# Cross attention: scaled negative queries, row minimum and exponential read from PSUM, eight score buffers, one loop over both head pairs

## The reference

```python
def memory_cross_attention(xn, memn, wq, wk, wv, wo):
    q = (xn @ wq).reshape(B, S, N_CROSS_HEADS, CROSS_HEAD_DIM)
    k = (memn @ wk).reshape(B, M, N_CROSS_HEADS, CROSS_HEAD_DIM)
    v = (memn @ wv).reshape(B, M, N_CROSS_HEADS, CROSS_HEAD_DIM)
    s = jnp.einsum('bshd,bmhd->bhsm', q, k) * (CROSS_HEAD_DIM ** -0.5)
    p = jax.nn.softmax(s, axis=-1)
    o = jnp.einsum('bhsm,bmhd->bshd', p, v).reshape(B, S, CROSS_WIDTH)
    return o @ wo
```

## Time and profile before

| | |
|---|---|
| median of 3 runs | 3515.47 us (3515.1 to 3517.26) |
| the profiled execution | 3516.87 us, its span 3515.6 us |
| TensorE busy, share of the span | 3219.0 us, 92% |
| VectorE, ScalarE, GpSimd busy | 42%, 29%, 21% |
| mean granted TensorE clock | 0.959 |

### The profile page before, as it was taken

How to read it: one execution, slowest core, us unless ns; L and a number is a source line. 1 busy time by engine, 2 the same in 40 slices (tenths; PEclk the granted TensorE clock), 3 DMA queues, 4 the chain that set the end, 5 groups by cost and what they waited for, 6 DMA issues and landing times.

```text
span 3515.6 us, 32414 instructions
## 1 busy us (share of the span) xinstructions
PE 3219.0 (92%) x12964; PEld 2212.1 (63%) x12964; DVE 1462.6 (42%) x2389; ACT 1023.5 (29%) x1679; POOL 752.2 (21%) x448
## 2 busy tenths in 40 slices
PE   6998888888899899999998799999988699999997
PEld 6444446655544788888886344486433488888886
DVE  4234443333217445545546544574223233333334
ACT  0223443334202222222223550063333422222223
POOL 0300002211005344444443110101000322222221
PEclk9999999989999999999999899999998799999998
DMA  6210001111114111111112102001300111111111
GB/s 199 84 31 24 24 30 32 41 36 54 72 61 149 36 60 48 48 48 48 48 48 81 39 24 74 30 3 44 108 24 25 53 54 48 48 48 48 48 48 54
DMA packets 195427, 187.25 MB, mean 53 GB/s; under 512 B 16119, under 2 KB 143503, under 8 KB 195279
## 3 DMA queue, kind: packets, MB, share of 16 engines
q1 hardware_dynamic: 195279, 185.19, 16.8%
HBM read 173.34 MB, written 9.70 MB: 52 GB/s over the span
## 4 chain that ended last, share of the span: by engine, by line
PE 82%; ACT 7%; DVE 6%; issue 3%; POOL 1%; SPq 1%; DMA 0%; POOLq 0%; ACTq 0%; DVEq 0%
PE bank L1026 62%; PE bank L1052 5%; PE bank L1122 2%; PE bank L1346 2%; PE bank L994 1%; PE bank L1330 1%; PE bank L1179 1%; PE bank L1300 1%; PE bank L1322 1%; PE bank L991 1%; PE bank L1188 1%; PE bank L989 1%; PE bank L1013 1%; PE bank L1389 1%; PE bank L1319 1%
## 5 line engine op out<-in xcount | busy, mean ns | idle before, releaser
L1026 PE MATMUL bank<-ft,panel 128*128 128x512 f32 x896 | 389.9, 596 | 7.5 <-ACT ft L2202 4.1
L1026 PEld LDWEIGHTS bank<-ft,panel 128*128 128x128 f32 x896 | 171.0, 192 | 222.9 <-issue 222.9
L1026 PE MATMUL bank<-ft_hi,panel_hi 128*128 128x512 f32 x704 | 278.2, 395 | 13.9 <-POOL ft_lo L2601 9.3
L1026 PE MATMUL bank<-ft_hi,panel_lo 128*128 128x512 f32 x704 | 278.4, 395 | 0.0
L1026 PE MATMUL bank<-ft_lo,panel_hi 128*128 128x512 f32 x704 | 277.4, 394 | 0.0
L2545 POOL TENSOR_TENSOR panel_lo<-panel,panelm_hi 128x1024 fp32r<-128x1024 f32 x64 | 153.1, 2393 | 508.1 <-ACT panelm_hi L2165 508.1
L1052 PE MATMUL bank<-ft,panel 128*128 128x512 f32 x512 | 245.0, 620 | 4.0 <-ACT z L2291 2.7
L1881 DVE TENSOR_SCALAR ffn_conv<-ffn_in,ffn_taps 128x512 f32<-128x512 f32 x88 | 113.0, 1284 | 316.1 <-ACT ffn_in L2408 316.1
L2132 DVE TENSOR_TENSOR resid<-resid,bank 128x512 f32<-128x512 f32 x256 | 174.5, 686 | 151.5 <-PE bank L1026 150.7
L1026 PE MATMUL bank<-ftm_hi,panelm_hi 128*128 128x512 f32 x512 | 203.3, 397 | 23.1 <-issue 12.9
L2545 POOL TENSOR_TENSOR panel_lo<-panel,panel_hi 128x1024 fp32r<-128x1024 f32 x66 | 157.9, 2400 | 248.0 <-ACT panel_hi L2165 248.0
(11 more groups left out here) (433 smaller groups left out, 5726.2 us busy)
## 6 DMA issues: line engine op xcount, KB each, us to landing
panel<-in_w_ada SPq DMA_DIRECT2D x48, 512.0 KB, 3.7
panel<-in_w_in SPq DMA_DIRECT2D x48, 512.0 KB, 3.7
panel<-in_ffn_w_up SPq DMA_DIRECT2D x44, 512.0 KB, 3.8
panel<-in_w_mlp_in SPq DMA_DIRECT2D x32, 512.0 KB, 4.1
panel<-in_w_mlp_out SPq DMA_DIRECT2D x32, 512.0 KB, 3.6
panel<-in_w_o SPq DMA_DIRECT2D x24, 512.0 KB, 3.6
panel<-in_w_out SPq DMA_DIRECT2D x24, 512.0 KB, 3.6
panel<-in_ffn_w_down SPq DMA_DIRECT2D x22, 512.0 KB, 3.5
```

Of the source, the lines that this page charges most:

```text
L1026: m = te.matmul(ps, a, b, start=(start and j == 0), stop=(stop and j == len(pairs) - 1))
```

## The change

The queries are multiplied by -1/sqrt(128) when they leave their banks, so the banks of `c_score` hold the negated, scaled scores. VectorE takes the row minimum directly from the bank, and this is the bias; the instruction that negated the maximum is gone. ScalarE's exponential reads the bank, with scale -1, writes the buffer and frees the bank; the instruction that copied and scaled the scores is gone. There are eight `c_scores` buffers. Scores are issued five steps ahead, finishes two steps ahead. Scores take banks 0 to 3, turns 4 and 5, weighings 6 and 7. The second half's scores and finishes are issued within the last steps of the first, and the first half's last weighing stands behind the turn of the second half's step 1.

```diff
@@ -40,6 +40,7 @@
 CROSS = 4
 NFF2 = 4096 // P
 AHEAD = 2
+C_AHEAD = 5
 SLOTS = 6
 SPLITS = 3
 
@@ -570,28 +571,35 @@
             k.unit("project", "cq", c, h, ps[c], used=ps[c], last=("cq", c, h))
             if h == 0 and c in (1, 2):
                 f3[c - 1]()
+
+    def c_score(i, u):
+        k.banks.take(("c_score", i, u), (0, 1, 2, 3))
+        k.unit("c_score", i, u, 2 * i + u // NT, u % NT)
+
+    def c_weigh(i, u):
+        k.banks.take(("c_weigh", i, u), (6, 7))
+        k.unit("c_weigh", i, u, 2 * i + u // NT, u // 4 % 2)
+
     for i in range(CROSS // 2):
-        def c_score(u):
-            k.banks.take(("c_score", i, u))
-            k.unit("c_score", i, u, 2 * i + u // NT, u % NT)
-
-        def c_weigh(u):
-            k.banks.take(("c_weigh", i, u))
-            k.unit("c_weigh", i, u, 2 * i + u // NT, u // 4 % 2)
-
-        for u in range(3):
-            c_score(u)
-        k.unit("c_finish", i, 0)
+        if i == 0:
+            for u in range(C_AHEAD):
+                c_score(i, u)
+            k.unit("c_finish", i, 0)
+            k.unit("c_finish", i, 1)
         for u in range(2 * NT):
-            if u < 2 * NT - 3:
-                c_score(u + 3)
-            if u < 2 * NT - 1:
-                k.unit("c_finish", i, u + 1)
-            k.banks.take(("c_turn", i, u))
+            later = (i, u + C_AHEAD) if u + C_AHEAD < 2 * NT else (i + 1, u + C_AHEAD - 2 * NT)
+            if later[0] < CROSS // 2:
+                c_score(*later)
+            soon = (i, u + 2) if u + 2 < 2 * NT else (i + 1, u + 2 - 2 * NT)
+            if soon[0] < CROSS // 2:
+                k.unit("c_finish", *soon)
+            k.banks.take(("c_turn", i, u), (4, 5))
             k.unit("c_turn", i, u)
             if u % 4 == 1 and u > 4:
-                c_weigh(u - 5)
-        c_weigh(2 * NT - 4)
+                c_weigh(i, u - 5)
+            elif u == 1 and i:
+                c_weigh(i - 1, 2 * NT - 4)
+    c_weigh(CROSS // 2 - 1, 2 * NT - 4)
     f1, a1 = feats("norm_mlp", range(4), ring), applies("norm_mlp", (0, 1, 2, 3))
     f2, a2 = feats("norm_mlp", (4, 5), ring), applies("norm_mlp", (4, 5))
     f3, a3 = feats("norm_mlp", (6, 7), ring), applies("norm_mlp", (6, 7))
@@ -696,7 +704,7 @@
     k.params, k.npar = place("params", [P, 4, 11]), place("npar", [P, 4, 2])
     k.lam, k.lam_sp = place("lam", [P, 8]), place("lam_sp", [P, 8])
     k.inv_freq = place("inv_freq", [P, 1])
-    k.c_stat = place("c_row_stat", [P, 4, 4])
+    k.c_stat = place("c_row_stat", [P, C_AHEAD + 3, 4])
     first_panel = top
     k.panels = [place(f"panel{n}", [P, D]) for n in range(SLOTS)]
     rows = top
@@ -802,7 +810,7 @@
     k.k_mem, k.v_mem = place("k_mem", [P, CROSS, MEM], at=late), place("v_mem", [P, MEM // P, BANK], at=late + 4 * D)
     k.mem_t, k.mem_ft = place("mem_t", [P, MEM // P, D], at=at(20)), place("mem_ft", [P, KD, MEM], at=at(22))
     top = at(12)
-    k.c_scores = [place(f"c_scores{n}", [P, MEM]) for n in range(4)]
+    k.c_scores = [place(f"c_scores{n}", [P, MEM]) for n in range(C_AHEAD + 3)]
     k.p_tc = [place(f"p_tc{n}", [P, MEM // P, BANK]) for n in range(2)]
 
 
@@ -1376,7 +1384,7 @@
         pe.wait_ge("c_weights_done", i, u)
         ps = free("c_turn", i, u)
         for kk in range(2):
-            m = te.transpose(ps[:, tile(kk)], k.c_scores[u % 4][:, tile(kk)], k.ident[:])
+            m = te.transpose(ps[:, tile(kk)], k.c_scores[u % len(k.c_scores)][:, tile(kk)], k.ident[:])
         fill(m, "c_turn", i, u)
 
     def c_weigh(i, u0, head, hf):
@@ -2087,15 +2095,13 @@
                                 ALU.add), "out_turn", pair, hf, 1)
 
     def c_score(i, u, head, n):
-        s, st = k.c_scores[u % 4], k.c_stat[:, u % 4, :]
+        st = k.c_stat[:, u % len(k.c_scores), :]
+        v.wait_ge(*v.filled("c_score", i, u))
+        dve.tensor_reduce(st[:, 0:1], v.bank("c_score", i, u)[:, 0:MEM], AX, ALU.min).then_inc(*v.new("c_least", i, u))
+
+    def c_finish(i, u):
+        st = k.c_stat[:, u % len(k.c_scores), :]
         v.wait_ge(*v.evicted("c_score", i, u))
-        dve.tensor_reduce(st[:, 0:1], s[:], AX, ALU.max).then_inc(*v.new("c_max", i, u))
-        v.wait_ge("c_max", i, u)
-        dve.tensor_scalar(st[:, 1:2], st[:, 0:1], -1.0, None, ALU.mult).then_inc(*v.new("c_bias", i, u))
-
-    def c_finish(i, u):
-        st = k.c_stat[:, u % 4, :]
-        v.wait_ge("c_exp", i, u)
         dve.reciprocal(st[:, 3:4], st[:, 2:3]).then_inc(*v.new("c_over", i, u))
 
     def c_turn(i, u):
@@ -2265,7 +2271,7 @@
             evict(act.activation(k.gate[h][:], ps[:], ACT.Silu), stage, c, h)
         elif stage == "cq":
             a.wait_ge(*a.filled(stage, c, h))
-            evict(act.copy(k.mix2[:, c, half(h)], ps[:]), stage, c, h)
+            evict(act.mul(k.mix2[:, c, half(h)], ps[:], -float(P) ** -0.5), stage, c, h)
 
     def ada_out(i, n, as_row):
         if as_row and i not in (GT_A, GT_F):
@@ -2488,16 +2494,16 @@
         evict(act.copy(k.k_mem[:, c, :], a.bank("ck", c)[:, 0:MEM]), "ck", c)
 
     def c_score(i, u, head, n):
-        s, st = k.c_scores[u % 4], k.c_stat[:, u % 4, :]
-        if i or u > 3:
-            a.wait_ge(*a.filled("c_turn", *((i, u - 4) if u > 3 else (i - 1, u + 12))))
-        a.wait_ge(*a.filled("c_score", i, u))
-        evict(act.mul(s[:], a.bank("c_score", i, u)[:, 0:MEM], float(P) ** -0.5), "c_score", i, u)
-        a.wait_ge("c_bias", i, u)
-        act.activation(s[:], s[:], ACT.Exp, bias=st[:, 1:2], accum_out=st[:, 2:3]).then_inc(*a.new("c_exp", i, u))
+        s, st = k.c_scores[u % len(k.c_scores)], k.c_stat[:, u % len(k.c_scores), :]
+        depth = len(k.c_scores)
+        if i or u >= depth:
+            a.wait_ge(*a.filled("c_turn", *((i, u - depth) if u >= depth else (i - 1, u + 2 * NT - depth))))
+        a.wait_ge("c_least", i, u)
+        evict(act.activation(s[:], a.bank("c_score", i, u)[:, 0:MEM], ACT.Exp, bias=st[:, 0:1], scale=-1.0,
+                             accum_out=st[:, 2:3]), "c_score", i, u)
 
     def c_finish(i, u):
-        s, st = k.c_scores[u % 4], k.c_stat[:, u % 4, :]
+        s, st = k.c_scores[u % len(k.c_scores)], k.c_stat[:, u % len(k.c_scores), :]
         a.wait_ge("c_over", i, u)
         act.activation(s[:], s[:], ACT.Copy, scale=st[:, 3:4]).then_inc(*a.new("c_weights_done", i, u))
 
```

## The result

| | before | after |
|---|---|---|
| median of 4 runs each, same chip | 3515.28 us (3514.61 to 3517.26) | 3469.27 us (3465.34 to 3471.08) |
| the profiled execution | 3516.87 us, span 3515.6 | 3471.08 us, span 3469.8 |
| first score to first w_co | 2601.70 to 2689.55, 87.85 us | 2600.34 to 2645.59, 45.25 us |
| behind it, to the end of the span | 826.05 us | 824.21 us |
| mean granted TensorE clock | 0.959 | 0.964 |

The ratio is 0.9867 [0.985, 0.9884]: 46.0 us less by the medians, 45.8 by the two profiled executions. Of these 45.8, 42.6 lie in the stage, 1.84 behind it and 1.36 ahead of it, where the kernels differ only in the scaling of the queries. Two more profiles of the kernel after start the stage at 2597.54 and 2601.78, so the 1.36 lies within what one kernel varies by.

A forecast was written before the change was run, and what follows sets the result against it. The cross attention stage was taken as bound by a chain of hand-overs, 1.93 us a step on ScalarE; 42.3 us off the stage plus 1.0 from the clock, 43.3 in total, gave 3473 us, range 3464 to 3486.

The forecast's parts named there:

- The round: In the cross attention's loop, four steps from one weighing to the next would take 5.17 us.
- The ends: Outside the stage's full rounds: 8.6 us to the first weighing, a last round of 4.67, an end of 6.4.
- The two unseen prices: In the stage, instructions reading PSUM that no earlier row showed: exponential taken at 0.50 us, minimum at 0.42.
- The cause of the wait: In each round, VectorE's copy of a weighing's result, waiting for TensorE, holds up the next minimum; round 0.88 us over TensorE's own.
- TensorE's 4.29: In the stage, TensorE's own need for four steps with their weighing at full clock: 4.29 us.
- Nor does a turn's bank: In the loop, turns' banks would not bind: turn 8 needs turn 6's copy, which ends ahead of multiplication 8.
- VectorE's 4.65: In the stage, VectorE's need for four steps, at most 4.65 us, with durations in place of distances.
- Rival 1: In the stage, TensorE is the bound: six rounds of 4.29 us, about 3466 us; chance 0.12.
- The clock: Behind the stage, mostly at w_co's start, denser TensorE work would win back 1.0 of up to 3.3 us.
- Rival 2: TensorE runs at the low clock level in the stage: rounds of 8.58 us, total 3498; chance 0.13.
- Rival 3: In the loop, hand-overs still alternate because only four banks hold scores: step 1.93 us, about 3515; chance 0.04.
- Rival 4: Slower: TensorE's low clock level lasts from the stage into w_co, about 3552 us if through all of it; chance 0.03.

The follow-up runs named there:

- experiment 4: The kernel after with VectorE's copy of a weighing's result issued a step later, behind the next minimum and next turn's copy: 3473.3 us, one execution.
- experiment 5: The kernel after with finishes issued three steps ahead instead of two: 3465.86 us, ratio 0.9858; on another chip 3464.55 us, ratio 0.9849.
- experiment 2: The kernel after with the old instructions (scaling copy, maximum, negation), so the new order alone: 3494.37 us, ratio 0.9945.
- experiment 1: The kernel before with the new instructions alone, keeping its old leads, four buffers and the break between the halves: 3482.61 us, ratio 0.991.
- experiment 3: The kernel after with the break between the halves put back, as two loops: 3470.04 us, ratio 0.9872.
- experiment 7: The kernel after with scores three steps ahead instead of five and six score buffers instead of eight: 3467.39 us, ratio 0.9858.

## Why the prediction was right

It said 3473.0 us; 3469.27 was measured, inside the range of 3464 to 3486 and on the side said likeliest.

**The stage.** 42.3 us less was said, 42.6 came. The round was said to take 5.17 and took 5.17. Term by term, predicted / measured in the timeline shown above: weighing to its copy 1.93 / 1.92; the copy 0.61 / 0.61; minimum to exponential 0.46 / 0.50; exponential, multiplication, exponential 1.40 / 0.47 + 0.40 + 0.45 = 1.32; multiplication to turn 0.56 / 0.55; turn to weighing 0.21 / 0.27. That the sum met to the digit is part luck: the hand-overs came out 0.08 longer and ScalarE's three instructions 0.08 shorter. The ends: first weighing 8.6 after the first score / 8.34; last round 4.67 / 4.72; end 6.4 / 6.31 (2639.28 to 2645.59).

**The two unseen prices.** The exponential from PSUM was kept at 0.50 and is 0.45 to 0.47 from start to start; the path has two in a round, and that is the 0.08 us that the hand-overs took back. The same 0.04 each explains the first weighing, 0.26 us earlier than said (nine exponentials, up to 0.36 us). The minimum from PSUM was taken at 0.42 and is 0.418 us; the same reduction from SBUF was 0.42 too. The added fixed time that the Trainium skill (VectorE: DVE Perf Modes, the TRN2 errata) gives, an estimate of 0.065 us by its figures, doesn't show in this instruction.

**The cause of the wait was named wrongly.** "... one wait stands in the order: VectorE's copy of a weighing's result stands ahead of the next minimum" is right for the order but not for the time. The prediction asked only when VectorE is free, not when the score is there. By its own rows the score can be read 1.73 + 0.69 = 2.42 us after the weighing's start, and VectorE is free at 1.93 + 0.61 = 2.54; so the copy cost 0.12 by the rows, and 0.18 in experiment 4, and most of the wait was TensorE's weighing, on its own engine. The sum was right because the two nearly coincide, which is luck. Whoever had mended the named cause would have lost 0.31 us a round; experiment 5, which mends the real one, takes 0.72 off.

**The engines' own needs.** TensorE's 4.29 is a little low or not at all: in experiment 5, where TensorE shows no idle time, a round takes 4.45, but 0.12 of it stands in the two steps whose turns still wait; the first two steps and the weighing run as said. "Nor does a turn's bank" held for the kernel after, and by those rows no longer holds with the finishes three ahead. VectorE's 4.65 was a bound from durations; from start to start its step is 0.72 (2611.21 to 2611.93 after), and with the copy of the result a round is 4 x 0.72 + 0.61 = 3.49. It was never near. Rival 1 with its six rounds of 4.29 is 1 us shorter than six rounds of experiment 5; its 3466 is nonetheless what experiment 5 gave, 3465.86 and 3464.55.

**The clock.** 1.0 us was said to be gained behind the stage, 1.84 was. In the first 20 us of w_co the clock was 0.89 and is 1.00, so (1 - 0.89) / 0.5 x 20 = 4.4 us were at the low level, half of it lost: 2.2 us, and the first result of w_co did come 2.14 us sooner. The prediction's upper end of 3.3 counted all low time from 2686 on; 3.55 us of that stretch, at a clock of 0.65, lie ahead of w_co, in the stage whose gain was already summed. What failed is the assumption that the idle time before w_co (0.98 us behind the copy of the result) would still cost part of the 2.2.

**The rivals.** Rival 2 (low level in the stage) didn't come: 1.00 over the whole stage, and 0.90 in experiment 2 and 0.94 in experiment 1, with their thinner stages. The Trainium skill (TensorE: Matmul & The Clock Gate, Part 4) says that the full clock doesn't engage for transposes. Here 64 of TensorE's 161 instructions in the stage are transposes, and the clock stayed at 1.00. That doesn't test the rule for transposes alone, since they hold only 4 x 0.21 of the 5.17 us of a round; mixed in so, they did no harm. Rival 3 (hand-overs that still alternate) is refuted by the waits, 8 instead of 32. Rival 4 has nothing in the rows for it; the 90 us shown have 0.79 after, 0.78 before.

**What was said to show it** came as said: distances 5.17 (5.2), ScalarE's wait once in four steps, VectorE's longest waits inside the loop those for the weighing, turns' waits 4.7 us (some 6).

## What to carry to other kernels

When a wait in a loop over in-order engines is put down to the instruction that stands ahead, work out for both sides when each is ready, the engine and the data: the later one is the cause, and here they lay 0.18 us apart, and moving the one that only seemed to block cost 0.31 us a round. The long instruction on one engine (a weighing of 1.7 us) was covered here by giving the follow-up work, the finishes, one more step of lead (0.72 us a round), and not by more lead or buffers for what feeds it (nothing). Before a difference of 1 to 3 us in a stage is read from whole times, look at that stage in the trace: here 3.0 us in the stage vanished in the rest.

## What the runs showed of the hardware

- **Reading PSUM was no dearer.** The 256-column reduction took 0.418 us from PSUM and 0.42 from SBUF, the exponential 0.468 from PSUM and 0.508 from SBUF.
- **The part behind the stage has a time of its own in each kernel.** Its code is the same in all, and two or three profiles of one kernel agree within 0.15 us (824.21, 824.31, 824.36 for the kernel after; 822.41, 822.46 for the earlier finishes), but kernels differ: 826.05 before, 821.31 to 821.51 in experiments 1, 3 and 7, 822.76 to 823.56 in the others. Between before and after, the difference arises in the first 18 us of w_co (2.14 us, shown above). Among the other kernels that stretch takes the same time (15.72 or 15.73 in the kernel after and in experiments 3 and 5); VectorE's first addition of an output of the layers behind (L2138 in the kernel after, L2133 in experiment 3) comes 152.25 us behind w_co's start in the kernel after, 149.34 in experiment 3 and 150.41 in experiment 5, so their difference arises between these two points. The granted clock in the 90 us shown goes the same way, though not in proportion: 0.79 after, 0.83 in experiment 3, and in experiment 5:

```profile
2691.49:2781.49 90.00, 65.81 (x242) 47.37 (x241) 19.50 (x49) 39.90 (x74) 31.00 (x22) 0.84 0.14 47
```

  What in the stage ahead decides which clock this stretch gets stays open; no run varied only that.
- **The part ahead of the stage varies from one execution to the next.** It took 2597.54, 2600.34 and 2601.78 us in three profiles of the kernel after, and 2597.45 and 2601.01 in two of the earlier finishes.
